# Half-row block ends, a spread gain row and other banks for the first gate unit, in a two-layer decoder on one core

## The chip, the cores and the metric

The kernel runs on one core of a Trainium2 chip. The metric is the device time in microseconds, from the launch of the program to its end; lower is better.

## What is computed

Two decoder layers on 256 tokens of width 1024, all weights read once from HBM in fp32. Layer 0 mixes with a state-space block, layer 1 with block attention on a shared K and V; each layer then has attention over 256 memory tokens and a gated feed-forward of width 2816.

```
x = x + rmsnorm(mixer(rmsnorm(x, mix_pre_g)), mix_post_g)
x = x + rmsnorm(memory_cross_attention(rmsnorm(x, mem_pre_g), mem_n, ...), mem_post_g)
x = x + rmsnorm(swiglu(rmsnorm(x, ffn_pre_g), w_gu, w_down), ffn_post_g)
```

So there are six places at which a product is normed, weighted with a post gain, added to x, and x is normed again with a pre gain for the next product. They are called block ends here: n = 0 to 5, behind w_out, wo0, down0, mo, wo1, down1. At n = 5 no second norm follows, and x goes out.

## The kernel before

The order on each engine is written out by hand, with semaphores between engines. Weights come in 1 MB units (128 x 2048 fp32) through a ring of four slots. For each unit SP issues the load when the unit four places back has been used (w_used), ScalarE rounds it to w_hi (L860), VectorE subtracts to w_lo (L1163, the weight remainder), and TensorE makes three products (hi x hi, hi x lo, lo x hi). Activations are split in the same way.

Tokens are two tiles of 128 (t = 0, 1). m_part() (L530) makes the product of a block end in banks 4 to 7, two banks of 512 columns for each token tile. The last two units are taken for tile 0 first, then for tile 1:

```
steps = [(i, t) for i in range(n - 2) for t in range(ST)] + [(i, t) for t in range(ST) for i in (n - 2, n - 1)]
```

norms() (L924) on ScalarE squares the product, sums it (statistic(), L880), and takes Ln and Exp. update() (L1219) on VectorE refines the inverse root in inverse_rms() (L1187), multiplies by it and by post_row (L1226), adds to x (L1229), raises x_ready, and calls normalise() (L1199), which needs the statistic of the new x and writes ntmp (L1205) for u_ready. TensorE transposes ntmp in turn() (L555, L567); ScalarE copies the result to actT_hi (L892) and VectorE makes actT_lo (L1213, raising turn_lo), and the next product waits for turn_lo (turn_done, L572).

While a block end runs, TensorE has fill work: units of the memory K and V of the same or the next layer, which do not depend on x. turn() takes one whole unit, the transposes of tile 0, half a unit, those of tile 1, and the other half. Ends 0 to 3 have two such units each, end 4 (wo1) has none. units_ahead() (L341) says how many units the engines prepare during an end: three, at end 4 two.

The feed-forward's gate and up units (pair_unit, L465) use two banks each, 0-1 for even and 2-3 for odd units, and loop_t() (L516) waits ahead of its loop until the two banks of the fill units have been copied out. A fill unit uses bank 0 or 1.

At the start SP loads both tiles of x, the first norm's gains spread over all partitions (512 KB written from 4 KB, into pre_row), the identity, and weights. TensorE runs dummy matmuls, warm() (L575), 40 before the first transposes and 24 behind them. d_pair is spread into par_rows on VectorE (L1249) ahead of the remainders of the first turn(). GpSimd issues the loads of later gain rows and, in the state-space part, sums squares. turn(1) (at L642) is the memory tokens' own norm, during the z units.

## Time and profile before

| | us |
|---|---|
| median of 3 runs (953.19 to 955.23) | 954.88 |
| the profiled execution: its time | 954.65 |
| its span, first to last instruction | 952.8 |
| TensorE busy in it | 921.3 |
| VectorE busy | 617.9 |
| ScalarE busy | 488.0 |
| mean granted TensorE clock, share of full speed | 0.990 |

The span is what the profile covers; 1.85 us of the execution's time lie around it. TensorE is the engine that is busy nearly always, so the time is its work and the gaps in it. The chain of work that ended last has 84% of the span on TensorE, 10% on VectorE and 4% on ScalarE. Idle time of the other engines matters only where TensorE waits for them.

### The profile page before, as it was taken

The numbers are of one execution on the slowest core, as the hardware profiler recorded it, in microseconds if no ns is written. First come the engines' busy times: TensorE is split into PE (matmuls) and PEld (weight loads), VectorE is DVE, ScalarE is ACT, GpSimd is POOL, SyncE is SP. The second block draws the span as 40 slices with busy tenths as digits, with TensorE's granted clock in tenths as the row PEclk, the third lists the DMA queues.
The fourth block names the chain that finished last, engine by engine and source line by source line (L and its number), as shares of the span: only waits on it lengthen the run. The fifth ranks groups of instructions, "written<-read, shape, count | busy, mean of one in ns | idle before, by whom it ended". The sixth has DMA issues, their size and how long they took to land.

```text
span 952.8 us, 14251 instructions
## 1 busy us (share of the span) xinstructions
PE 921.3 (97%) x5920; PEld 820.1 (86%) x5920; DVE 617.9 (65%) x689; ACT 488.0 (51%) x654; POOL 55.2 (6%) x67
## 2 busy tenths in 40 slices
PE   8999999999999999999999999999999599999996
PEld 6999998878899888888888999987998488888885
DVE  6788466895754677777643854675854657777533
ACT  5565467664555554444434644656645634444332
POOL 1000003450000000000000220000000000000000
PEclk9999999999999999999999999999999799999999
DMA  8756544225652555555555796434643345555551
GB/s 265 264 181 190 160 142 131 100 94 177 201 196 89 177 179 195 195 180 176 182 214 177 227 281 202 132 112 133 221 151 110 115 153 196 180 176 182 205 186 44
DMA packets 121060, 163.77 MB, mean 172 GB/s; under 512 B 4077, under 2 KB 106917, under 8 KB 121013
## 3 DMA queue, kind: packets, MB, share of 16 engines
q1 hardware_dynamic: 117684, 151.99, 48.8%
q0 software_dynamic: 3328, 11.10, 3.8%
q8 instruction: 35, 0.57, 0.3%
q14 instruction: 13, 0.10, 0.0%
HBM read 162.01 MB, written 1.07 MB: 171 GB/s over the span
## 4 chain that ended last, share of the span: by engine, by line
PE 84%; DVE 10%; ACT 4%; issue 1%; DMA 1%; SPq 0%; DVEq 0%; ACTq 0%
PE bank L450 49%; PE bank L471 18%; PE bank L473 9%; DVE w_lo L1163 2%; DVE ntmp L1226 1%; PE bank L772 1%; PE bank L743 1%; DVE x L1229 1%; DVE ntmp L1205 1%; ACT ntmp L882 1%; PE bank L661 1%; PE bank L567 1%; DMA d_pair<-in_ssm_d_dram 1%; DVE stats L1194 1%; DVE stats L1196 1%
## 5 line engine op out<-in xcount | busy, mean ns | idle before, releaser
L1163 DVE TENSOR_TENSOR w_lo<-w_raw,w_hi 128x2048 fp32r<-128x2048 f32 x135 | 308.7, 2292 | 134.8 <-ACT w_hi L860 134.1
L860 ACT ACTIVATE w_hi<-w_raw 128x2048 fp32r<-128x2048 f32 x135 | 257.3, 1913 | 207.6 <-DMA w_raw<-in_ffn_w_gu_dram 102.4
L471 PE MATMUL bank<-actT,w_hi 128*128 128x512 f32 x704 | 250.6, 401 | 2.6 <-DVE actT L1213 1.6
L450 PE MATMUL bank<-actT,w_hi 128*128 128x256 f32 x1152 | 209.3, 284 | 0.8 <-DVE w_lo L1174 0.5
L473 PE MATMUL bank<-actT,w_lo 128*128 128x256 f32 x704 | 198.4, 282 | 0.0
L450 PEld LDWEIGHTS bank<-actT,w_hi 128*128 128x128 f32 x1152 | 179.6, 192 | 2.3 <-issue 1.3
L471 PEld LDWEIGHTS bank<-actT,w_hi 128*128 128x128 f32 x704 | 133.1, 189 | 36.4 <-issue 3.1
L450 PE MATMUL bank<-actT,w_lo 128*128 128x256 f32 x576 | 163.0, 283 | 0.0
L473 PEld LDWEIGHTS bank<-actT,w_lo 128*128 128x128 f32 x704 | 133.9, 190 | 0.0
L450 PEld LDWEIGHTS bank<-actT,w_lo 128*128 128x128 f32 x576 | 110.5, 192 | 0.0
L450 PE MATMUL bank<-w_hi,hT_hi 128*128 128x512 f32 x176 | 68.5, 389 | 0.0
L450 PE MATMUL bank<-w_lo,hT_hi 128*128 128x512 f32 x176 | 68.5, 389 | 0.0
L450 PE MATMUL bank<-w_hi,hT_lo 128*128 128x512 f32 x176 | 68.5, 389 | 0.0
L450 PE MATMUL bank<-w_hi,actT 128*128 128x512 f32 (+1 forms) x256 | 64.1, 339 | 0.0
L1429 DVE TENSOR_REDUCE hval<-bank 128x512 f32<-128x1024 f32 x22 | 26.9, 1224 | 44.0 <-PE bank L473 44.0
L450 PEld LDWEIGHTS bank<-w_hi,actT 128*128 128x128 f32 x256 | 44.3, 190 | 5.4 <-issue 0.3
L450 PE MATMUL bank<-w_lo,actT 128*128 128x512 f32 (+1 forms) x128 | 43.0, 336 | 0.0
L450 PEld LDWEIGHTS bank<-w_hi,hT_lo 128*128 128x128 f32 x176 | 33.0, 188 | 7.0
L450 PEld LDWEIGHTS bank<-w_hi,hT_hi 128*128 128x128 f32 x176 | 33.0, 188 | 6.9
L450 PEld LDWEIGHTS bank<-w_lo,hT_hi 128*128 128x128 f32 x176 | 33.0, 188 | 6.8
L450 PE MATMUL bank<-w_hi,memT_hi 128*128 128x256 f32 x128 | 37.2, 290 | 0.0
L450 PE MATMUL bank<-memT_hi,w_hi 128*128 128x256 f32 x128 | 37.2, 290 | 0.0
(209 smaller groups left out, 1334.2 us busy)
## 6 DMA issues: line engine op xcount, KB each, us to landing
w_raw<-in_ffn_w_gu_dram SPq DMA_DIRECT2D x44, 1024.0 KB, 5.0
w_raw<-in_ffn_w_down_dram SPq DMA_DIRECT2D x22, 1024.0 KB, 4.9
w_raw<-in_ssm_w_in_dram SPq DMA_DIRECT2D x20, 1024.0 KB, 5.3
w_raw<-in_mem_w_kv_dram SPq DMA_DIRECT2D x16, 1024.0 KB, 5.3
w_raw<-in_ssm_w_out_dram SPq DMA_DIRECT2D x8, 1024.0 KB, 4.9
w_raw<-in_mem_w_q_dram SPq DMA_DIRECT2D x8, 1024.0 KB, 5.0
w_raw<-in_mem_w_o_dram SPq DMA_DIRECT2D x8, 1024.0 KB, 4.9
w_raw<-in_w_kv_dram SPq DMA_DIRECT2D x8, 1024.0 KB, 6.5
```

The source lines that it names most:

```text
L450: ins = pe.matmul(dst, a, b, start=first and n == 0, stop=last and n == len(passes) - 1, skip_group_check=True)
L471: pe.matmul(bank[:, b + c, :], wh, actT[:, k].rearrange("p e n -> p (e n)"), start=k == 0, stop=False, skip_group_check=True)
L473: ins = pe.matmul(bank[:, b + c, S:2 * S], wl, actT_hi[:, k, :], start=False, stop=k == KD - 1, skip_group_check=True)
L567: ins = pe.transpose(bank[:, 4 + 2 * t + half, q * P:(q + 1) * P], ntmp[:, t, c:c + P], ident)
L661: pe.matmul(bank[rows, 3 + j % 2 * 3, 0:S], xtok[:, j % 3, 0, rows], mt[:, j % 3, e, 0:S], start=True, stop=False, skip_group_check=True)
L743: ins = pe.matmul(bank[:, b, t * S:(t + 1) * S], qT[:, 2 * h + kk, t * P:(t + 1) * P], memK[:, 2 * h + kk, :], start=kk == 0, stop=kk == 1 ...
L772: ins = pe.matmul(bank[:, 2 + h % 2, d * S:(d + 1) * S], memV[:, m, c:c + P], probT[:, h % 2, m, :], start=m == 0, stop=m == 1, skip_group ...
L860: act.activation(hi[:, u % SLOTS, :], raw[:, u % SLOTS, :], ACT.Copy).then_inc(w_hi_done, 1)
L882: act.activation(ntmp[:, t, :], src, ACT.Square, accum_out=stats[:, 0, c:c + 1]).then_inc(sum_ready, 1)
L1163: dve.tensor_tensor(lo[:, s, :], raw[:, s, :], hi[:, s, :].bitcast(F32), ALU.subtract).then_inc(w_lo_done, 1)
L1194: own.mark(dve.scalar_tensor_tensor(out=step, in0=r, scalar=v, in1=r, op0=ALU.mult, op1=ALU.mult))
L1429: dve.tensor_reduce(dst[:, b], halves, AX.X, ALU.add).then_inc(t_out["dve"], 1)
```

## The change

- m_part: the last two units are taken in four quarters (tile 0 left half of the columns, tile 0 right half, tile 1 left, tile 1 right) of 12 matmuls each. m_quarter is raised behind the first three, w_used in the last.
- ScalarE: each square is done in two halves of 512 columns; the first half's sum goes through an added Identity, which gives its mean plus eps, and enters Ln as the bias. The copies of tile 0's transposes now stand ahead of the statistic of x of tile 1, and the third prepared unit behind all.
- VectorE: the product times post_row is made half by half, before the scale is known; one operation per half then multiplies by the scale and adds x. The remainders of tile 0's transposes stand ahead of the second norm of tile 1, and the third weight remainder behind it.
- turn on TensorE: half a unit of fill, tile 0, two halves of fill, tile 1, half a unit; the transposes wait half by half.
- The first norm's gains come as one row on one partition. Two matmuls with a row of ones spread them into banks 0 and 1, where the first norm reads them. The dummy matmuls are 24, 16 and 16. first_row and ones_row overlie conv_acc in the shared region, which stays at its address.
- d_pair is spread on GpSimd.
- Gate and up units use banks 2-3 for even and 0-1 for odd units. The wait for the last fill unit's copy is at the second unit.
- x is stored in four pieces of 256 KB, not in two of 512.
- At end 4 the table load for silu stands ahead of the last copies, not behind them.

Counts on x_ready, u_ready and sum_ready follow the halves. In the diff, removed lines of m_part, norms and the copy of d_pair, which the listing above has, are left out.

```diff
-WARM = [10, 6]
+WARM = [6, 4, 4]
...
+        first_row, _ = shared("first_row", [P, D], F32, 0)
+        ones_row, _ = shared("ones_row", [P, P], F32, 4096)
...
+        def sums_in(c, half):
+
+            return c + 1 if c < 4 else 2 * (c - 4) + 5 + half
...
             for t in range(ST):
                 sp.dma_start(x[:, t, :], A["x"][0, t * P:(t + 1) * P, :]).then_inc(x_loaded[t], 16)
-            sp.dma_start(pre_row[:], every_row(TURN_GAIN[0])).then_inc(pre_first, 16)
+                if t == 0:
+                    sp.dma_start(first_row[0:1, :], TURN_GAIN[0].unsqueeze(0)).then_inc(row_loaded, 16)
             sp.dma_start(const[:, 0:P], A["consts"][:, 0:P]).then_inc(ident_loaded, 16)
             load(0)
...
-                sp.wait_ge(x_ready, 2 * len(POST_GAIN) - 1 + t)
-                sp.dma_start(out[0, t * P:(t + 1) * P, :], x[:, t, :]).then_inc(stored, 16)
-            sp.wait_ge(stored, 16 * ST)
+                for half in range(2):
+                    sp.wait_ge(x_ready, 4 * (len(POST_GAIN) - 1) + 2 * t + half + 1)
+                    cols = slice(half * 512, half * 512 + 512)
+                    sp.dma_start(out[0, t * P:(t + 1) * P, cols], x[:, t, cols]).then_inc(stored, 16)
+            sp.wait_ge(stored, 16 * 2 * ST)
...
+            pool.wait_ge(par_loaded, 64)
+            d_rows = slice(D_ROW, D_ROW + XT)
+            pool.tensor_copy(par_rows[d_rows, 1, :].rearrange("c (e n) -> c e n", e=2), d_pair[d_rows, :].unsqueeze(2).broadcast_to([XT, 2, HD])).then_inc(consts_made, 1)
+            pool.wait_ge(u_ready, 4)
...
-                    pair_unit(u % SLOTS, i % 2 * 2).then_inc(w_used, 1)
+                    pair_unit(u % SLOTS, 2 - i % 2 * 2).then_inc(w_used, 1)
...
-                for e, n in FREED[v0 - 2:v0]:
-                    pe.wait_ge(t_out[e], n)
                 with pe.Fori(0, iters) as i:
                     for j in range(5):
+                        if j == 1:
+                            e, n = FREED[v0 - 1]
+                            pe.wait_ge(t_out[e], n)
                         if j:
                             pe.wait_ge(t_out["dve"], i * 4 + (d0 + j - 1))
                         if j < 4:
                             pe.wait_ge(w_lo_done, i * 4 + (u0 + j + 1))
-                            pair_unit((u0 + j) % SLOTS, j % 2 * 2).then_inc(w_used, 1)
+                            pair_unit((u0 + j) % SLOTS, 2 - j % 2 * 2).then_inc(w_used, 1)
...
+                def part(i, t, half, r):
+
+                    u, k = U[(name, i)], i * MR + r
+                    ah, al = act_hi[:, k, t * P:(t + 1) * P], act_lo[:, k, t * P:(t + 1) * P]
+                    cols = slice(r * D + half * 512, r * D + half * 512 + 512)
+                    wh, wl = hi[:, u % SLOTS, cols], lo[:, u % SLOTS, cols]
+                    return product(bank[:, 4 + 2 * t + half, :], [(ah, wh), (ah, wl), (al, wh)], k == 0, k == n * MR - 1)
+
+                for i in range(n - 2):
+                    ready(i)
+                    pe.wait_ge(w_lo_done, U[(name, i)] + 1)
+                    for t in range(ST):
+                        if t and i == 0 and last_y:
+                            last_y()
+                        for r in range(MR):
+                            for half in range(2):
+                                ins = part(i, t, half, r)
+                    ins.then_inc(w_used, 1)
+                for t in range(ST):
+                    for half in range(2):
+                        for i in (n - 2, n - 1):
+                            if t == 0 and half == 0:
+                                ready(i)
+                                pe.wait_ge(w_lo_done, U[(name, i)] + 1)
+                            for r in range(MR):
+                                ins = part(i, t, half, r)
+                            if t and half:
+                                ins.then_inc(w_used, 1)
+                        if not (t and half):
+                            ins.then_inc(m_quarter, 1)
...
-                if name:
-                    fill(name, i)
                 for t in range(ST):
-                    if name and t:
-                        fill_half(name, i + 1, 0)
-                    pe.wait_ge(u_ready, 2 * k + t + 1)
+                    if name:
+                        if t:
+                            fill_half(name, i, 1)
+                        fill_half(name, i + t, 0)
                     for half in range(2):
+                        pe.wait_ge(u_ready, 4 * k + 2 * t + half + 1)
                         for q in range(4):
                             c = (half * 4 + q) * P
...
+            pe.wait_ge(row_loaded, 16)
+            for half in range(2):
+                product(bank[:, half, :], [(ones_row[0:1, :], first_row[0:1, half * 512:(half + 1) * 512])], True, True).then_inc(pre_first, 1)
+            warm(WARM[1])
...
+            def statistic_halves(c, t, src, *ready):
+
+                first, first_mean = small[:, 2 + t:3 + t], small[:, 4 + t:5 + t]
+                for half, (s, count) in enumerate(ready):
+                    cols = slice(half * 512, half * 512 + 512)
+                    act.wait_ge(s, count)
+                    act.activation(ntmp[:, t, cols], src[:, cols], ACT.Square,
+                                   accum_out=stats[:, 0, c:c + 1] if half else first).then_inc(sum_ready, 1)
+                    act.wait_ge(sum_ready, sums_in(c, half))
+                    if half == 0:
+                        own.mark(act.activation(first_mean, first, ACT.Identity, bias=eps_col, scale=1.0 / D))
+                own.wait()
+                own.mark(act.activation(stats[:, 1, c:c + 1], stats[:, 0, c:c + 1], ACT.Ln, bias=first_mean, scale=1.0 / D))
+                own.wait()
+                act.activation(stats[:, 2, c:c + 1], stats[:, 1, c:c + 1], ACT.Exp, scale=-0.5).then_inc(stat_ready, 1)
...
-                act.wait_ge(m_half, n + 1)
-                hi_upto(last + 2)
+                statistic_halves(stat_col(n, 0, 0), 0, msum[0], (m_quarter, 3 * n + 1), (m_quarter, 3 * n + 2))
+                if units_ahead(n) > last + 2:
+                    hi_upto(last + 2)
                 if POST_TURN[n] is not None:
-                hi_upto(units_ahead(n))
+                    statistic_halves(stat_col(n, 0, 1), 0, x[:, 0, :], (x_ready, 4 * n + 1), (x_ready, 4 * n + 2))
+                statistic_halves(stat_col(n, 1, 0), 1, msum[1], (m_quarter, 3 * n + 3), (w_used, last + 1))
                 if POST_TURN[n] is not None:
+                    turn(POST_TURN[n], actT_hi, [0])
+                    statistic_halves(stat_col(n, 1, 1), 1, x[:, 1, :], (x_ready, 4 * n + 3), (x_ready, 4 * n + 4))
+                if units_ahead(n) > last + 2:
+                    hi_upto(units_ahead(n))
...
-                act.preload_act_table_set("silu_and_others")
+                if layer == 0:
+                    act.preload_act_table_set("silu_and_others")
...
             norms(4)
-            turn(7, actT_hi)
+            act.preload_act_table_set("silu_and_others")
+            turn(7, actT_hi, [1])
...
+                t = (c - 4) % 4 // 2 if c < 24 else c - 24
+                total0, v0 = small[:, 2 + t:3 + t], small[:, 6 + t:7 + t]
+                dve.wait_ge(sum_ready, sums_in(c, 0))
+                if c < 4:
+                    own.mark(dve.tensor_scalar(v, total, -0.5 / D, -0.5 * EPS, ALU.mult, ALU.add))
+                else:
+                    own.mark(dve.tensor_scalar(v0, total0, -0.5 / D, -0.5 * EPS, ALU.mult, ALU.add))
+                    if gains:
+                        gains(0)
+                    dve.wait_ge(sum_ready, sums_in(c, 1))
+                    own.wait()
+                    own.mark(dve.tensor_scalar(v, total, -0.5 / D, v0, ALU.mult, ALU.add))
+                    if gains:
+                        gains(1)
...
-                dve.scalar_tensor_tensor(out=ntmp[:, t, :], in0=src[:, t, :], scalar=stats[:, 5, c:c + 1],
-                                         in1=pre_row[:], op0=ALU.mult, op1=ALU.mult).then_inc(u_ready, 1)
-
-            def turn(k, dst_hi, dst_lo):
-                for t in range(ST):
+                    dve.wait_ge(*((pre_loaded, 16 * k) if k else (pre_first, 2)))
+                for half in range(2):
+                    cols = slice(half * 512, half * 512 + 512)
+                    dve.scalar_tensor_tensor(out=ntmp[:, t, cols], in0=src[:, t, cols], scalar=stats[:, 5, c:c + 1],
+                                             in1=pre_row[:, cols] if k else bank[:, half, :], op0=ALU.mult, op1=ALU.mult).then_inc(u_ready, 1)
+
+            def turn(k, dst_hi, dst_lo, tokens=range(ST)):
...
+                    def gains(half):
+
+                        cols = slice(half * 512, half * 512 + 512)
+                        own.mark(dve.tensor_tensor(ntmp[:, t, cols], bank[:, 4 + 2 * t + half, :], post_row[:, cols], ALU.mult))
+
+                    inverse_rms(c, gains)
+                    for half in range(2):
+                        cols = slice(half * 512, half * 512 + 512)
+                        dve.scalar_tensor_tensor(out=x[:, t, cols], in0=ntmp[:, t, cols], scalar=stats[:, 5, c:c + 1],
+                                                 in1=x[:, t, cols], op0=ALU.mult, op1=ALU.add).then_inc(x_ready, 1)
+                    if t and POST_TURN[n] is not None:
+                        turn(POST_TURN[n], actT_hi, actT_lo, [0])
+                    if t == 0 and units_ahead(n) > last_unit(M_OF_POST[n]) + 2:
+                        lo_upto(last_unit(M_OF_POST[n]) + 2)
                     if POST_TURN[n] is not None:
                         normalise(POST_TURN[n], stat_col(n, t, 1), t, x)
+                if units_ahead(n) > last_unit(M_OF_POST[n]) + 2:
+                    lo_upto(units_ahead(n))
...
-            dve.wait_ge(par_loaded, 64)
...
+            lo_upto(U[("mq", 1)])
...
```

Place 1, VectorE, block end 0, tile 1 of the tokens from the sum of the product to the new x. Before:

```order
L1191 TENSOR_SCALAR stats<-stats 128x1 [waits sum_ready]
L1194 SCALAR_TENSOR_TENSOR stats<-stats 128x1 [waits stat_ready,dve_step]
L1196 TENSOR_SCALAR stats<-stats 128x1 [waits dve_step]
L1226 SCALAR_TENSOR_TENSOR ntmp<-bank,stats,post_row 128x1024 [waits dve_step]
L1229 TENSOR_TENSOR x<-x,ntmp 128x1024 [waits dve_step]
L1163 TENSOR_TENSOR w_lo<-w_raw,w_hi 128x2048 [waits w_hi_done]
```

After:

```order
L1241 TENSOR_SCALAR small<-small 128x1 [waits sum_ready]
L1288 TENSOR_TENSOR ntmp<-bank,post_row 128x512
L1246 TENSOR_SCALAR stats<-stats,small 128x1 [waits dve_step,sum_ready]
L1288 TENSOR_TENSOR ntmp<-bank,post_row 128x512
L1251 SCALAR_TENSOR_TENSOR stats<-stats 128x1 [waits stat_ready,dve_step]
L1253 TENSOR_SCALAR stats<-stats 128x1 [waits dve_step]
L1293 SCALAR_TENSOR_TENSOR x<-ntmp,stats,x 128x512 [waits dve_step]
L1293 SCALAR_TENSOR_TENSOR x<-ntmp,stats,x 128x512
L1272 TENSOR_TENSOR actT<-bank,actT 128x4x128 [waits turn_hi] x2
```

The two operations of 1024 columns have become four of 512, of which the two on post_row no longer wait for the scale (stat_ready). The weight remainder (w_lo) is gone from here, and the remainders of tile 0's transposes have come in behind x.

Place 2, VectorE, what follows there: the second norm of tile 1 and the remainders of the transposes. Before:

```order
L1191 TENSOR_SCALAR stats<-stats 128x1 [waits sum_ready]
L1194 SCALAR_TENSOR_TENSOR stats<-stats 128x1 [waits stat_ready,dve_step]
L1196 TENSOR_SCALAR stats<-stats 128x1 [waits dve_step]
L1205 SCALAR_TENSOR_TENSOR ntmp<-x,stats,pre_row 128x1024 [waits dve_step]
L1213 TENSOR_TENSOR actT<-bank,actT 128x4x128 [waits turn_hi] x4
```

After:

```order
L1241 TENSOR_SCALAR small<-small 128x1 [waits sum_ready]
L1246 TENSOR_SCALAR stats<-stats,small 128x1 [waits dve_step,sum_ready]
L1251 SCALAR_TENSOR_TENSOR stats<-stats 128x1 [waits stat_ready,dve_step]
L1253 TENSOR_SCALAR stats<-stats 128x1 [waits dve_step]
L1264 SCALAR_TENSOR_TENSOR ntmp<-x,stats,pre_row 128x512 [waits dve_step]
L1264 SCALAR_TENSOR_TENSOR ntmp<-x,stats,pre_row 128x512
L1208 TENSOR_TENSOR w_lo<-w_raw,w_hi 128x2048 [waits w_hi_done]
L1272 TENSOR_TENSOR actT<-bank,actT 128x4x128 [waits turn_hi] x2
```

The weight remainder that stood ahead of this norm now stands between it and the last two remainders of the transposes.

Place 3, TensorE, the start of the program (cum is a tile of zeros, const the identity). Before:

```order
L577 UNCONDITIONAL_BRANCH [waits zeros_made]
L579 MATMUL bank<-cum_102 128x256 x4
L577 REGISTER_ALU
L577 COMPARE_AND_BRANCH
L567 MATMUL bank<-const,ntmp 128x128 [waits u_ready,ident_loaded]
L567 MATMUL bank<-const,ntmp 128x128 x7
L567 MATMUL bank<-const,ntmp 128x128 [waits u_ready]
L567 MATMUL bank<-const,ntmp 128x128 x7
L588 MATMUL bank<-const,par_rows 128x128 [waits consts_made]
```

After:

```order
L603 MATMUL bank<-cum_104 128x256 x4
L601 REGISTER_ALU
L601 COMPARE_AND_BRANCH
L463 MATMUL bank<-first_row,ones_row 128x512 [waits row_loaded]
L463 MATMUL bank<-first_row,ones_row 128x512
L601 UNCONDITIONAL_BRANCH
L603 MATMUL bank<-cum_104 128x256 x4
L601 REGISTER_ALU
L601 COMPARE_AND_BRANCH
L591 MATMUL bank<-const,ntmp 128x128 [waits u_ready,ident_loaded]
L591 MATMUL bank<-const,ntmp 128x128 x3
L591 MATMUL bank<-const,ntmp 128x128 [waits u_ready]
```

Two matmuls on the row of gains stand among the dummy ones, and the transposes wait once per half row.

## Rows read from the trace of the kernel before

**Rows 1.** The page, part 1: engine, busy us, share, instructions.

```profile
PE 921.3 (97%) x5920; PEld 820.1 (86%) x5920; DVE 617.9 (65%) x689; ACT 488.0 (51%) x654; POOL 55.2 (6%) x67
```

**Rows 2.** The waits of TensorE: us in total, times, longest.

```profile
PE bank L567 <- DVE ntmp L1205: 16.8, 9, 5.1
...
PE bank L471 <- ACT memK L913: 1.0, 1, 1.0
```

**Rows 3.** Timeline, first block end: start us, us, engine, line, names, idle before.

```profile
238.33 2.29 DVE L1163 TENSOR_TENSOR w_lo<-w_raw,w_hi 128x2048 fp32r<-128x2048 f32 x1 [3.21 <-ACT w_hi L860]
...
247.76 1.03 ACT L882 ACTIVATE ntmp<-bank 128x1024 f32<-128x1024 f32 x1 [2.25 <-PE bank L450]
...
248.90 0.15 DVE L1191 TENSOR_SCALAR stats<-stats 128x1 f32<-128x1 f32 x1 [2.38 <-ACT ntmp L882]
...
252.50 2.29 DVE L1163 TENSOR_TENSOR w_lo<-w_raw,w_hi 128x2048 fp32r<-128x2048 f32 x1
...
253.00 0.28 PE L450 MATMUL bank<-w_hi,memT_hi 128*128 128x256 f32 x1
...
255.39 1.28 DVE L1205 SCALAR_TENSOR_TENSOR ntmp<-x,stats,pre_row 128x1024 f32<-128x1024 f32 x1
...
258.75 1.03 PE L567 MATMUL bank<-const,ntmp 128*128 128x128 f32 x8
...
263.96 1.09 PE L567 MATMUL bank<-const,ntmp 128*128 128x128 f32 x8 [1.31 <-DVE ntmp L1205]
```

**Rows 4.** Timeline of TensorE, first gate unit of the first layer.

```profile
344.07 0.49 PE L471 MATMUL bank<-actT,w_hi 128*128 128x512 f32 x1 [0.97 <-ACT memK L913]
```

**Rows 5.** Timeline of TensorE, block end of wo1 (no fills).

```profile
748.35 1.68 PE L567 MATMUL bank<-const,ntmp 128*128 128x128 f32 x8 [3.11 <-DVE ntmp L1205]
755.12 1.97 PE L567 MATMUL bank<-const,ntmp 128*128 128x128 f32 x8 [5.10 <-DVE ntmp L1205]
758.67 0.79 PE L471 MATMUL bank<-actT,w_hi 128*128 128x512 f32 x1 [1.58 <-DVE actT L1213]
```

**Rows 6.** Timeline of the tail, and one window: busy by engine, clock, DMA, GB/s.

```profile
944.88 1.02 ACT L882 ACTIVATE ntmp<-bank 128x1024 f32<-128x1024 f32 x1 [3.76 <-PE bank L450]
...
948.48 1.23 DVE L1229 TENSOR_TENSOR x<-x,ntmp 128x1024 f32<-128x1024 f32 x1
...
949.74 0.36 SPq L386 DMA_DIRECT2D out_dram<-x  x1
...
951.00:952.00 1.00, 0.00 (x0) 0.00 (x0) 0.00 (x0) 0.00 (x0) 0.00 (x0) 0.50 0.86 348
```

**Rows 7.** Timeline and one window of the start, and timeline round turn(1).

```profile
6.64 0.21 DVE L1196 TENSOR_SCALAR stats<-stats 128x1 f32<-128x1 f32 x1
...
7.96 1.28 DVE L1205 SCALAR_TENSOR_TENSOR ntmp<-x,stats,pre_row 128x1024 f32<-128x1024 f32 x1 [1.11 <-DMA pre_row<-in_mix_pre_g_dram]
...
9.39 1.07 PE L567 MATMUL bank<-const,ntmp 128*128 128x128 f32 x8 [1.82 <-DVE ntmp L1205]
...
12.00:15.00 3.00, 3.00 (x17) 2.43 (x16) 2.76 (x6) 2.58 (x4) 0.00 (x0) 0.53 1.10 337
...
12.21 0.22 DVE L1249 COPY par_rows<-d_pair 16x128 f32<-16x128 f32 x1 [1.08 <-DMA d_pair<-in_ssm_d_dram]
...
17.27 0.50 PE L450 MATMUL bank<-actT,w_hi 128*128 128x256 f32 x2 [0.48 <-DVE w_lo L1174]
...
114.90 1.09 PE L567 MATMUL bank<-const,ntmp 128*128 128x128 f32 x8 [0.73 <-DVE ntmp L1205]
...
123.36 0.48 PE L450 MATMUL bank<-actT,w_hi 128*128 128x256 f32 x2 [0.33 <-DVE w_lo L1163]
```

**Rows 8.** Groups by shape: count, busy us, mean ns, idle before.

```profile
L1213 DVE TENSOR_TENSOR actT<-bank,actT 128x512 fp32r<-128x512 f32 x28 | 17.9, 684 | 2.4 <-ACT actT L892 2.3
...
L892 ACT ACTIVATE actT<-bank 128x512 fp32r<-128x512 f32 x28 | 15.2, 597 | 12.4 <-PE bank L567 12.4
...
L424 POOL TENSOR_TENSOR ysum<-ysum,ysq 128x256 f32<-128x256 f32 x12 | 14.1, 1177 | 0.9
```

80 lines of the change are left out of this document (22 added, 58 removed).

## The prediction

> **What bounds the kernel now.** I read five views in this order: the page, the waits of TensorE, the timeline round each place where TensorE waited, the windows with the granted clock, and the groups by shape. The page has TensorE busy for 921.3 us of a span of 952.8 [rows 1]. The matmuls themselves are the same before and after the change, so what it can win is in the remaining 31.5 us, plus the stretches in which TensorE counts as busy on dummy matmuls or at half clock. The waits say where that idle time is: 16.8 us in nine waits for the normalised rows that turn() transposes, and 1.0 us for a copy out of bank 1 [rows 2]. The rest is the first microseconds, the last ones, and scraps.
>
> The timeline of the first block end shows what such a wait is made of [rows 3]. ScalarE squares token tile 0 at 247.76, and VectorE has the sum at 248.90. Then come VectorE's scaled row, the addition, and the weight remainder of a prefetched unit (2.29), and only then the normalised row at 255.39. Token tile 1 goes through the same chain behind it. TensorE arrives with its fill work done and stands 1.31 us at 263.96. The same 1.31 us recur at the three other block ends that have fill work: with 1.82 and 0.73 at the start, 0.73 at turn(1) and the 3.11 and 5.10 below, four of 1.31 make up the 16.8 us.
>
> Where there is no fill work (before the second feed-forward) the chain is bare: waits of 3.11, 5.10 and 1.58 us [rows 5]. At the very end nothing covers it either [rows 6].
>
> **Prices.** An elementwise VectorE operation of 512 columns takes 0.68 us and a ScalarE one 0.60 [rows 8]; of 1024 columns they take 1.28 and 1.03 [rows 3]. Halving therefore costs about 0.08 us extra on VectorE for each cut where operations follow without a wait, and I use 0.74 for a half with a scalar operand (0.68 and a little, as the scalar form stands 0.05 above the other at 1024 columns: 1.28 against 1.23 [rows 3, 6]). The sum of the last half row comes 0.43 us sooner than that of a whole row (1.03 less 0.60): 0.72 us after the square starts, against 1.14 [rows 3].
>
> **A block end with fills (four of them).** I count from the moment at which the last square of tile 0 can start, 247.76 in rows 3. Before, the post-gain product and the addition were two 1024-column operations behind the statistic. Now the gain product runs while ScalarE does Ln and Exp, and one fused operation per half finishes x. VectorE: sum 0.72, gain product of the second half to 1.5, two Newton steps to 2.0, x halves ready at 2.75 and 3.4. Then the weight remainder, which keeps its place, to 5.6, the second norm's scalars to 6.4, and the normalised halves at 7.1 and 7.8. TensorE reaches tile 0's transposes after the rest of its matmuls (253.00, which is 5.24) and now only half a unit of fill, 2.87 (a whole one took from 253.00 to 258.75 [rows 3]): at 8.1. So it waits for nothing, with 1.0 us to spare.
>
> Tile 1 on VectorE: two gain halves, scalars and x to 11.2, the two remainders of tile 0's transposes to 12.4, scalars to 13.3, and the first half of the normalised row at 14.1. TensorE is there at 8.1 + 1.05 + 5.75 = 14.9. The 1.31 us wait goes, with 0.8 us to spare. What is late next: the weight remainder that the change puts behind this row (2.29) stands on VectorE ahead of the last two remainders of the transposes, which end at 18.2. TensorE has finished its last half unit at 18.8. Spare 0.6 us. That unit's load is released some 1.3 us later than before (half a quarter), because unit n-2 now ends in the last quarter; the remainder made of it stands some 10 us behind the release. The last unit's own remainder is needed 1.3 us earlier too, 4 us before 247.4, and it was done at 240.6 [rows 3]. **4 x 1.31 = 5.2 us gained.** Bounds: 0 (spare used up) and 5.2, since TensorE can't gain more than it waited.
>
> **First gate unit in other banks.** It no longer waits for the copy of k1's second unit. That wait was 0.97 [rows 4]. About 0.1 of it is loop entry that stays. **0.85 us gained**, bounds 0.5 and 0.97. For the second layer there is no such copy, so nothing. One wait now stands inside the loop; its value is long reached, so it costs nothing.
>
> **The block end without fills.** The same chain from 739.8: normalised tile 0 at 746.1 and 746.8 instead of 748.3; tile 1's halves at 753.1 and 753.8 instead of 755.07. TensorE is at half clock here, 1.97 us for eight transposes against 1.07 at the start [rows 5, 7], and I leave that so, since it idles between the tiles as long as before. The last four transposes end at 754.9, copy and remainder add 1.4, and the first gate matmul starts at 756.55 against 758.67. The moved table load falls into a wait. **2.1 us gained**, bounds 1.3 and 3.
>
> **The tail.** From the square at 944.88 the last half of x is done at 948.3, against 949.71, when the whole row was [rows 6]. The last store then carries 256 KB, not 512, and the store moved 348 GB/s: 0.75 us less. **2.15 us gained**, bounds 1.4 (store no shorter) and 2.3.
>
> **The start.** VectorE had the scale of tile 0 at 6.85 and stood until 7.96 for the row of gains on all partitions [rows 7]. Now 4 KB are loaded, one place earlier in SP's queue, and two matmuls spread them into banks 0 and 1, between 24 and 16 dummy matmuls; before there were 40. Normalised halves at 7.6 and 8.3, tile 1's at 9.6 and 10.3. Then the remainders, which stood behind the copy of d_pair until 12.4 [rows 7], run from 10.2 to 12.7. Weight halves on both engines follow, and the first real matmul could start at 15.1 instead of 17.27. The copy of d_pair goes to GpSimd, behind four DMA issues and that same load. It cost 0.22 on VectorE [rows 7]; on GpSimd I bound it by 0.22 and 1.18 [rows 8] and take 0.5. If d_pair lands as before (12.2), par_rows are turned at 13.2, 16 dummy matmuls end at 15.3, and the first real matmul is at 15.4. I take that: **1.9 us gained**, bounds 0 and 2.3.
>
> **The middle.** turn(1) waited 0.73 for tile 1 of mem and 0.33 later for a remainder [rows 7]. The first shrinks, but the second is the end of a ScalarE and VectorE chain from the same starting point, which the halving lengthens: **0.1 us lost**, bounds 0.3 lost and 0.3 gained. Elsewhere the queue of SP is not changed. On GpSimd the gain rows' DMAs wait for the same events in other counts, and the new copy stands only ahead of a DMA that waits until w_used 3.
>
> **Sum.** 5.2 + 0.85 + 2.1 + 2.15 + 1.9 - 0.1 = 12.1. The profiled execution took 954.65 us, the median of the runs shown is 954.88, within their spread. 954.65 - 12.1 = **942.6 us**.
>
> **Rivals.**
> 1. The start gives nothing. The par_rows transposes and dummy matmuls stand on TensorE ahead of the first real one, and GpSimd may reach the copy late. TensorE's clock is at stake too: it ran at 0.53 of full speed from 12 to 15 [rows 7], after TensorE had stood 1.82 us at 9.39. Now it may stand behind tile 1 instead, and a fall that came three microseconds later would lie on real matmuls. For 3.4 us at half speed that costs 1.7. Against it: less idle time in all. Time: 942.6 + 1.9, up to + 3.6: 944.5 to 946.2. The Trainium skill (TensorE: Matmul & The Clock Gate, What's actually happening) has the throttled clock as the default and activity as what releases it; by that, moving the idle time moves the slow stretch, as this rival has it.
> 2. The waits come back at the block ends: the half of the fill that now stands behind tile 0's transposes no longer covers them, or VectorE's last remainders come after the fill. A spare of 0.6 to 1.0 us is small against a chain of some 20 operations. If each operation there is 0.1 us longer than I have it, each of the four ends loses up to 1.2 us: 942.6 + 4.8 = 947.4 at most, 945 likely.
> 3. Slower than before. VectorE's chain per end has eleven operations that are now half rows. If a half row costs e more than 0.74 us, TensorE waits 11e - 0.6 at each of four ends, 11e at the fifth, and the tail grows by 3e: 58e - 2.4 in all. This eats the gain of 12.1 from e = 0.25, a half row at 0.99 us. At e = 0.5, where a half costs nearly what a whole row does, the time is 954.65 - 12.1 + 26.6 = 969. Against it: 28 such operations at 0.684 [rows 8]; for it only that the fused form with x as both input and output, and a product straight from PSUM, are not in the trace at this width. The Trainium skill (VectorE: DVE Perf Modes, The TRN2 errata) speaks against such cuts: each instruction pays a fixed latency that a large tile pays once. Its formula for fp32 tensor_tensor gives 0.69 us at 512 columns, beside the row's 0.684, so by it e is zero.
> 4. The change does little of what it says: a wait that ended last at the four ends and in the feed-forward comes back as another one of the same length, and only tail and start remain: 954.65 - 4.05 = 950.6. For it: three engines take part in each end and the trace shows only the wait that ended last. One part of the change's name does nothing in any case: no tile after the new ones has another address.
>
> **How the numbers follow.** My forecast 0.62, rival 1 0.15, rival 2 0.15, rival 3 0.03, rival 4 0.03, and 0.02 for no change at all. The range runs down to 940.5 (all terms at their better bound) and up to 947.2, where rivals 1 and 2 end. What lies outside is the far part of rival 2, rival 3, rival 4, and my own terms if several are off the same way: 2 in 10. About 0.2% (1.9 us) is what a measurement here can tell from no change. Faster 0.95, same 0.02, slower 0.03.
>
> **What would show it.** In the profile after: no wait for the normalised row above 0.2 us at the four ends, first gate matmul straight behind its fill, first gate matmul of layer two about 2 us sooner after the last one of wo1, last store under 2.5 us before the span's end, first real matmul at 15.4. VectorE's half rows must stand at 0.68 to 0.75. If they stand at 0.9 or more, or TensorE waits for turn_lo, I am wrong in rivals 3 or 2.

## The result, and the profile after

The changed kernel took 943.16 us (median of four runs, 940.91 to 945.87) beside 955.06 for the kernel before (four runs, 953.19 to 955.90): a ratio of 0.9889, 95% interval 0.9867 to 0.9911 (the two medians by themselves give 0.9875). I had forecast 942.6. The profiled execution took 943.9, 10.75 less than the one before; its span is 942.1. The sum agrees, and yet two of its terms were far off, and an effect that it did not have made up for most of that.

The page, part 1, and the waits of TensorE, which answer to [rows 1] and [rows 2] (us in total, times, longest):

```profile
PE 920.4 (98%) x5916; PEld 819.3 (87%) x5916; DVE 624.7 (66%) x751; ACT 499.6 (53%) x720; POOL 55.6 (6%) x68
```

```profile
PE bank L591 <- DVE ntmp L1264: 7.6, 4, 5.8
PE bank L463 <- DVE w_lo L1219: 2.1, 1, 2.1
...
PE bank L484 <- DVE actT L1272: 1.6, 1, 1.6
```

Nine waits of 16.8 us for the normalised row have become four of 7.6. The 1.0 for memK is gone, and the wait for a weight remainder ahead of the first real matmul has grown from 0.48 [rows 7] to 2.06. The timeline of the first block end (start us, us, engine, line, names, idle before), to be held against [rows 3]:

```profile
247.58 0.60 ACT L914 ACTIVATE ntmp<-bank 128x512 f32<-128x512 f32 x1 [1.39 <-PE bank L463]
...
254.20 1.42 DVE L1264 SCALAR_TENSOR_TENSOR ntmp<-x,stats,pre_row 128x512 f32<-128x512 f32 x2
...
255.69 1.03 PE L591 MATMUL bank<-const,ntmp 128*128 128x128 f32 x8
...
261.36 1.42 DVE L1264 SCALAR_TENSOR_TENSOR ntmp<-x,stats,pre_row 128x512 f32<-128x512 f32 x2
...
262.31 1.16 PE L591 MATMUL bank<-const,ntmp 128*128 128x128 f32 x8
```

Neither group of transposes has idle time in front, where the second had 1.31. But the eight transposes of tile 1 took 1.16 us, those of tile 0 1.03: the second half row came at 262.8 and the last four waited for it a little. At the ends 2 and 3 it is 1.32; before the change it was 1.09 at all four. The gate units, the end without fills and the tail, against [rows 4 to 6]:

```profile
340.32 0.49 PE L484 MATMUL bank<-actT,w_hi 128*128 128x512 f32 x1
...
740.51 1.32 PE L591 MATMUL bank<-const,ntmp 128*128 128x128 f32 x8 [1.10 <-DVE ntmp L1264]
747.67 1.97 PE L591 MATMUL bank<-const,ntmp 128*128 128x128 f32 x8 [5.83 <-DVE ntmp L1264]
751.22 0.79 PE L484 MATMUL bank<-actT,w_hi 128*128 128x512 f32 x1 [1.59 <-DVE actT L1272]
...
936.11 0.60 ACT L914 ACTIVATE ntmp<-bank 128x512 f32<-128x512 f32 x1 [1.70 <-PE bank L463]
...
938.96 0.99 SPq L396 DMA_DIRECT2D out_dram<-x  x2
```

Two stores are one row there; the second was issued at 939.63, 2.48 us before the span's end (before: 3.08). The start, against [rows 7]:

```profile
1.74 4.92 PE L603 MATMUL bank<-cum 128*128 128x256 bf16 x24 [1.74 <-DVE small L1314]
6.59 1.98 PE L463 MATMUL bank<-first_row,ones_row 1*128 1x512 f32 x4
...
7.09 1.06 ACT L926 ACTIVATE ntmp<-x 128x1024 f32<-128x1024 f32 x1 [1.11 <-DMA x<-in_x_dram]
...
8.68 1.41 DVE L1264 SCALAR_TENSOR_TENSOR ntmp<-x,stats,bank 128x512 f32<-128x512 f32 x2 [2.12 <-PE bank L463]
...
16.83 0.51 PE L463 MATMUL bank<-actT,w_hi 128*128 128x256 f32 x2 [2.06 <-DVE w_lo L1219]
```

VectorE stood 2.12 us, not for a DMA but for the two products that spread the row. They are four records, 1.98 us, and they began only when 24 dummy matmuls had ended at 6.59.

Laid over each other, the two profiles give the gain stage by stage. The same event came sooner by 0.44 us at the first real matmul (17.27, now 16.83) and 0.18 at the first square of the first block end (247.76, 247.58), so the middle lost 0.26. At the last wo1 matmul it is 5.82 (744.85, 739.03): less 0.18, and less 0.9 for the first gate unit, the four ends with fills gave 4.7. When VectorE begins to reduce layer two's first gate unit it is 6.51 (766.26, 759.75): 0.69 for the end without fills. At the last of layer two's 22 gate and up units it is **8.75** (884.98, 876.23): 2.24 us came from the gate loop, in which the matmuls and their order were not changed, only the banks. The tail gave 1.94.

That loop is the surprise. VectorE reduces each unit when TensorE has finished it. After the change, the reductions of the third and the twenty-first unit of layer one, and of the first and the last unit of layer two:

```profile
357.72 1.22 DVE L1497 TENSOR_REDUCE gate<-bank 128x512 f32<-128x1024 f32 x1
...
459.48 1.22 DVE L1497 TENSOR_REDUCE gate<-bank 128x512 f32<-128x1024 f32 x1
...
759.75 1.22 DVE L1497 TENSOR_REDUCE gate<-bank 128x512 f32<-128x1024 f32 x1 [3.16 <-PE bank L486]
...
876.23 1.23 DVE L1497 TENSOR_REDUCE hval<-bank 128x512 f32<-128x1024 f32 x1 [1.89 <-PE bank L486]
```

The same four in the kernel before:

```profile
361.46 1.22 DVE L1429 TENSOR_REDUCE gate<-bank 128x512 f32<-128x1024 f32 x1
...
463.22 1.21 DVE L1429 TENSOR_REDUCE gate<-bank 128x512 f32<-128x1024 f32 x1
...
766.26 1.22 DVE L1429 TENSOR_REDUCE gate<-bank 128x512 f32<-128x1024 f32 x1 [3.41 <-PE bank L473]
...
884.98 1.22 DVE L1429 TENSOR_REDUCE hval<-bank 128x512 f32<-128x1024 f32 x1 [2.09 <-PE bank L473]
```

Layer one: (459.48 - 357.72) / 18 is 5.65 us a unit, and so is (463.22 - 361.46) / 18. Layer two: (876.23 - 759.75) / 21 is 5.55, where (884.98 - 766.26) / 21 is 5.65. A unit has 16 pairs of one 512-column and one 256-column matmul; the time from pair to pair, 353.3 or 346.7 ns, is called the slow and the quick rhythm below.

### The profile page after: what moved, and what is told of

Same layout as the page of the kernel before. It is cut to its first block, busy times and chain, and to the rows that moved or that the text cites. A ratio compares the mean times of both kernels' runs of the same rounds, so it can differ in the third digit from the quotient of the medians.

```text
span 942.1 us, 14413 instructions
## 1 busy us (share of the span) xinstructions
PE 920.4 (98%) x5916; PEld 819.3 (87%) x5916; DVE 624.7 (66%) x751; ACT 499.6 (53%) x720; POOL 55.6 (6%) x68
## 3 DMA queue, kind: packets, MB, share of 16 engines
q0 software_dynamic: 3328, 11.10, 3.6%
## 4 chain that ended last, share of the span: by engine, by line
PE 87%; DVE 7%; ACT 3%; issue 2%; DVEq 0%; ACTq 0%
PE bank L463 51%; PE bank L484 18%; PE bank L486 9%; DVE conv_acc L1378 2%; DVE w_lo L1208 2%; PE bank L800 1%; PE bank L771 1%; PE bank L591 1%; PE bank L689 1%; DVE ntmp L1264 1%; PE bank L603 1%; PE bank L854 1%; PE bank L844 0%; PE bank L727 0%; ACT w_hi L888 0%
```

## The experiments

Unless an edit says otherwise, each is made in the changed kernel, so it is compared with 943.16 (and with the 942.65 of the first experiment). A ratio is that to the kernel before, run beside it.

**1. The same kernel again.** No edit.

> The changed kernel, nothing altered. In its profile 32 matmuls of a gate unit came in pairs 346.7 ns apart in the second layer's gate loop and 353.3 ns apart in the first layer's (before the change: 353.3 in both). That is 0.106 us a unit, 2.2 us over the 21 units, which no term of my sum has. Theory A (the rhythm is set by the program: by the bank order or by how TensorE comes out of the half clock there): the pairs stand again at 353 in the first and 347 in the second layer, and the total within 1 us of 943.2. Theory B (the rhythm is a state that an execution falls into by the instant at which the loop is entered): the profile shows another combination, 347/347 or 353/353, with a span 2.2 us shorter or longer by it, and the single times spread over 4 to 5 us as before (940.9 to 945.9), in steps of about 2.2.

Measured: 942.65 us (six runs, 940.53 to 946.19), ratio 0.9883 (0.9858 to 0.9908). Its units took 5.55 us in both layers: theory B, as far as the combination changed; that the instant of entry picks it is not shown. Its start and its clock differ from the first profile too. The window is: busy by engine, granted clock, DMA share, GB/s.

```profile
17.23 0.54 PE L463 MATMUL bank<-actT,w_hi 128*128 128x256 f32 x1 [2.06 <-DVE w_lo L1219]
```

```profile
17.30:20.70 3.40, 3.40 (x16) 3.40 (x17) 2.01 (x5) 3.40 (x2) 0.00 (x0) 0.50 0.84 231
744.40:754.50 10.10, 5.87 (x20) 4.90 (x21) 7.36 (x12) 8.50 (x11) 0.45 (x1) 0.50 0.21 76
```

After 2.06 us of idle time the clock fell to the lower of its two levels (0.50, 1.2 GHz) just as the first real matmuls began. From there to the wait behind turn(1) this execution took 107.81 us, the first one 106.35: 1.5 us given away. My rival 1 described this; of the eight profiles with this start it happened in this one alone. The second window is the end without fills: there the clock was back at full 10.24 us after its fall, where the first profile needed 13.65. From the last wo1 matmul to the reduction of the first gate unit this execution took 19.87 us, the first one 20.72.

**2. The spread ahead of the dummy matmuls.** WARM counts them in groups of four.

```
-WARM = [6, 4, 4]
+WARM = [2, 8, 4]
...
-                if t == 0:
-                    dve.wait_ge(*((pre_loaded, 16 * k) if k else (pre_first, 2)))
+                if t == 0 and k:
+                    dve.wait_ge(pre_loaded, 16 * k)
                 for half in range(2):
+                    if t == 0 and not k:
+                        dve.wait_ge(pre_first, half + 1)
```

> The two matmuls that spread the row of gains stand behind 8 dummy matmuls, not 24 (then 32 more), and each half of tile 0 waits for its own half of the row. My theory: the start missed 1.5 of the 1.9 us I gave it because VectorE stood 2.12 us for the spread, which began at 6.59 behind dummy matmuls at half clock and took 1.98. By it VectorE starts the normalised row at 6.6 to 7.1 instead of 8.68 and the first real matmul is at 15.3 to 15.9 instead of 16.83, if tile 1 isn't last; where tile 1 of x is (it landed at 7.09, its scale at 9.2), the gain is smaller, about 0.9: 15.9. Rival: the row itself lands late, the spread can't start before 5.5, and the products run at half clock at 3.4 us for four: the normalised row at 8.5 or later, the first real matmul where it was, 16.8, or later. In us: 942.3 (mine), 943.2 or slower (rival).

Measured: 943.78 us (five runs, 943.76 to 945.48), ratio 0.9894. The rival's time, and a start worse than it had it:

```profile
4.13 3.78 PE L463 MATMUL bank<-first_row,ones_row 1*128 1x512 f32 x4 [0.52 <-DMA first_row<-in_mix_pre_g_dram]
7.83 5.84 PE L603 MATMUL bank<-cum 128*128 128x256 bf16 x32
13.51 1.91 PE L591 MATMUL bank<-const,ntmp 128*128 128x128 f32 x16
...
19.61 0.50 PE L463 MATMUL bank<-actT,w_hi 128*128 128x256 f32 x2 [2.22 <-DVE w_lo L1219]
```

The row had landed by 4.13, so the DMA is not late. But the four records took 3.78 us at the lower clock, and the clock rose only at 12.32 (in the thirteen other profiles of this study between 4.4 and 7.4). 32 dummy matmuls, most of them at half clock, then stood in front of tile 0's transposes. The start lost 2.8 us against the first profile; the total hardly moved because both gate loops of this profile had the quick rhythm, worth 2.2. Before the clock rose, TensorE had run 8 dummy matmuls, stood idle 0.52 us, run the four one-row products, and then run dummy matmuls for 4.5 us. The Trainium skill (TensorE: Matmul & The Clock Gate, What's actually happening) makes activity the thing that releases the clock; the trace agrees in so far as the rise came while matmuls ran. Why it came so late here this one profile does not show.

**3. The row loaded onto all partitions again.**

```
-WARM = [6, 4, 4]
+WARM = [10, 0, 4]
...
-                if t == 0:
-                    sp.dma_start(first_row[0:1, :], TURN_GAIN[0].unsqueeze(0)).then_inc(row_loaded, 16)
+            sp.dma_start(pre_row[:], every_row(TURN_GAIN[0])).then_inc(row_loaded, 16)
...
-            pe.wait_ge(row_loaded, 16)
-            for half in range(2):
-                product(bank[:, half, :], [(ones_row[0:1, :], first_row[0:1, half * 512:(half + 1) * 512])], True, True).then_inc(pre_first, 1)
-            warm(WARM[1])
...
```

> The start undone but for the copy on GpSimd: the row of gains is loaded onto all partitions in the third place of the queue, 40 dummy matmuls in one piece, no spread. My theory, by which the spread and the copy's move between them gave 0.44 us: VectorE starts the normalised row at about 8.0, so 0.7 sooner than with the spread, but the second tile and par_rows come from the queue behind 512 KB; first real matmul at 17.0 plus or minus 0.3, so +0.2 us against the change. Rival (the spread cost more than it saved): 16.3 or sooner, 0.5 us faster than the change. Second rival (the move of the copy cost what the spread gave): above 17.3.

Measured: 942.29 us (five runs, 940.38 to 945.78), ratio 0.9872, no different from the change. VectorE and TensorE:

```profile
8.47 0.75 DVE L1259 SCALAR_TENSOR_TENSOR ntmp<-x,stats,pre_row 128x512 f32<-128x512 f32 x1 [1.76 <-DMA pre_row<-in_mix_pre_g_dram]
```

```profile
16.64 0.38 PE L462 MATMUL bank<-actT,w_hi 128*128 128x256 f32 x1 [1.30 <-DVE w_lo L1214]
```

The first real matmul came between what my theory and the first rival said: the spread neither saves nor costs anything that can be told (16.64 against 16.83 and 17.23 in the two profiles of the change, whose clock also rose later). By elimination the start owes its gain to the rest, the half rows and the copy of d_pair off VectorE; no run parts these two.

**4. TensorE kept busy at the end without fills.** The matmuls stand in turn(7), between the two tiles.

```
+                    if t and busy:
+                        stay_busy(busy)
...
+            def stay_busy(n):
+
+                with pe.Fori(0, n):
+                    for _ in range(4):
+                        pe.matmul(bank[:, 2, 0:S], const[:, 0:P // 2].bitcast(BF16), const[:, 0:P].bitcast(BF16), start=True, stop=True,
...
-            turn(7)
+            turn(7, busy=11)
```

> 44 dummy matmuls (128 x 256, bf16) between the transposes of tile 0 and tile 1 at the block end without fills, where TensorE stands 5.83 us and its clock is at half from 743.44 to 757.09. At 0.12 us each, as at the start, they take 5.3 us of the 5.8. Theory A (the idle time makes the clock fall, and half a clock on the first nine pairs of the gate unit is what took back the gain of that end): the clock stays at full, eight transposes take 1.05 instead of 1.97 us, nine pairs save 0.29 us each, 2.7 us, and the first gate matmul is about 1.0 us sooner: 3.6 us faster, 939.6. Theory B (the clock falls all the same, or the dummy matmuls come in the way of the transposes): no gain or up to 1 us lost. Beside it, on the rhythm of the pairs in the second layer: if what makes it 347 ns is the way out of the half clock, it is 353 here, and 2.2 us of the gain go, 941.8.

Measured: **938.81 us** (six runs, 937.33 to 945.25), ratio 0.9843 (0.9813 to 0.9873); beside it experiment 1 had 942.65.

```profile
740.70 4.97 PE L602 MATMUL bank<-const 128*128 128x256 bf16 x44
746.70 1.32 PE L593 MATMUL bank<-const,ntmp 128*128 128x128 f32 x8 [1.03 <-DVE ntmp L1273]
749.60 0.49 PE L484 MATMUL bank<-actT,w_hi 128*128 128x512 f32 x1 [1.58 <-DVE actT L1281]
```

```profile
743.50:757.00 13.50, 10.88 (x71) 9.07 (x70) 10.90 (x15) 9.86 (x14) 0.53 (x1) 1.00 0.24 80
```

Theory A. From the last wo1 matmul to the first gate unit's reduction it takes 17.38 us (738.07 to 755.45), where the change took 20.72 in its first profile and 19.87 in its second: 3.3 or 2.5 gained. The rhythm in the second layer stayed the quick one, so it does not come from leaving the lower clock. One of the six runs took 945.25 at a mean clock of 0.994, the others had 0.999. The later experiments 9 to 11 have this edit too, and there the clock still fell, for 3.41 us.

**5. Gate matmuls grouped.**

```
                     for k in range(KD):
                         cols = slice(k * TC + c * P, k * TC + (c + 1) * P)
-                        wh, wl = hi[:, slot, cols], lo[:, slot, cols]
-                        pe.matmul(bank[:, b + c, :], wh, actT[:, k].rearrange("p e n -> p (e n)"), start=k == 0, stop=False,
+                        pe.matmul(bank[:, b + c, :], hi[:, slot, cols], actT[:, k].rearrange("p e n -> p (e n)"), start=k == 0, stop=False,
                                   skip_group_check=True)
-                        ins = pe.matmul(bank[:, b + c, S:2 * S], wl, actT_hi[:, k, :], start=False, stop=k == KD - 1,
+                    for k in range(KD):
+                        cols = slice(k * TC + c * P, k * TC + (c + 1) * P)
+                        ins = pe.matmul(bank[:, b + c, S:2 * S], lo[:, slot, cols], actT_hi[:, k, :], start=False, stop=k == KD - 1,
                                         skip_group_check=True)
```

> In a gate unit the eight 512-column matmuls of a half stand first and the eight 256-column ones behind them, where the changed kernel lets them alternate. Five profiles so far show the alternating pair at either 353.3 or 346.7 ns, in each layer by itself: 353/347, 347/347, 347/347, 353/353, 353/347. Runs of equal matmuls elsewhere stand at 226.7 and 120 ns, 346.7 together. Theory A (the slow rhythm belongs to the alternation, and which one an execution has is chance of the instant): grouped, every unit takes 16 x 0.3467 = 5.55 us in both layers, the single times lie within 2 us where they lay over 5 to 6, and the median is 1 to 2 us below the 942.7 of the unaltered kernel. Theory B (the slow rhythm is in the loop, its loads or VectorE's and ScalarE's use of the banks): 5.65 us a unit still turns up in some layer, and the spread stays.

Measured: 943.1 us (six runs, 941.41 to 944.01), ratio 0.9893. The spread halved from 5.7 us to 2.6, the median did not move. Two units in a row took 11.17 us throughout, 5.587 each: behind every change from 256 to 512 columns the next few matmuls take up to 9 ns more each. That lies between the two rhythms of the alternating form (5.547, 5.654), so theory A holds for the cause and not for the gain. Over the twelve profiles of alternating kernels, before and after, 12 layers had the quick rhythm and 12 the slow one.

**6. Banks of the gate units as before.**

```
-                    pair_unit(u % SLOTS, 2 - i % 2 * 2).then_inc(w_used, 1)
+                    pair_unit(u % SLOTS, i % 2 * 2).then_inc(w_used, 1)
...
+                for e, n in FREED[v0 - 2:v0]:
+                    pe.wait_ge(t_out[e], n)
                 with pe.Fori(0, iters) as i:
                     for j in range(5):
-                        if j == 1:
...
```

> The banks of the gate units as before the change: the first gate unit of layer one writes banks 0 and 1 and waits for the copy of k1's second unit out of bank 1. My theory: that wait comes back at 0.9 to 1.0 us in layer one, nothing in layer two, so 0.9 us slower than the change by the profile's stages. Rival (the new order of the last half units has moved the copy out of the way, so the wait is hidden anyway): 0.3 or less. Second rival (bank order, not the wait, makes the quick rhythm of the second layer): pairs at 353 ns in both layers, 2.2 us slower.

Measured: 944.37 us (four runs, 941.84 to 945.94), ratio 0.9897.

```profile
340.46 0.49 PE L484 MATMUL bank<-actT,w_hi 128*128 128x512 f32 x1 [0.97 <-ACT memK L956]
```

The wait is back at its old 0.97. From the first real matmul to the reduction of the twenty-first unit this profile took 443.54 us, the change 442.65: 0.89, as forecast. Its rhythm is slow in both layers, as the second rival has it, but so was that of experiment 3 with the new banks; one profile does not settle it.

**7. The whole fill unit ahead of tile 0 again.**

```
-                    if name:
-                        if t:
-                            fill_half(name, i, 1)
-                        fill_half(name, i + t, 0)
+                    if name and t == 0:
+                        fill_half(name, i, 0)
+                        fill_half(name, i, 1)
+                    elif name:
+                        fill_half(name, i + 1, 0)
```

> The fill work at the four ends stands as before the change (a whole unit ahead of tile 0's transposes, half a unit between the tiles, half behind), all half rows stay. TensorE's matmuls and their number are the same. Theory A (the gain of the ends needs the earlier transposes of tile 0, because ScalarE copies them ahead of tile 1's second square): from A, the square of tile 0, TensorE is at tile 0's transposes at +11.1 instead of +8.1, ScalarE's two copies end at +12.9, the squares, Ln and Exp of tile 1 behind them at +14.8, and tile 1's normalised half at +15.9, where TensorE arrives at +14.7: 1.2 to 1.9 us waited at each of the four ends, 5 to 7 us slower in all. Theory B (shorter links alone make the gain, and the place of the fill doesn't matter): no wait above 0.3, same time as the change.

Measured: 951.08 us (ten runs, 948.62 to 954.23), ratio 0.9969 (0.9952 to 0.9987): some 8 us slower. ScalarE and TensorE:

```profile
258.43 1.09 ACT L937 ACTIVATE actT<-bank 128x512 fp32r<-128x512 f32 x2 [4.42 <-PE bank L592]
259.40 0.63 ACT L915 ACTIVATE ntmp<-x 128x512 f32<-128x512 f32 x1
```

```profile
263.05 1.32 PE L592 MATMUL bank<-const,ntmp 128*128 128x128 f32 x8 [1.35 <-DVE ntmp L1265]
```

Theory A. ScalarE's copies of tile 0 stand ahead of tile 1's second square, and behind a late transpose they push it. 1.35 us of wait return here, and each of the four ends is 1.35 to 1.65 us longer by the stages, 6.1 in all: more than the 4.7 that the four ends had gained. Half rows with TensorE's old order lose there, while ScalarE keeps its new one, with the copies ahead of the second square; half rows with both old orders were not run. The rest of the 8 us I can't place; its gate loops ran slow and quick like the change's.

**8. One more half-row product ahead of x of tile 1.**

```
                     inverse_rms(c, gains)
+                    if t:
+                        gains(1)
+                        own.wait()
```

> One more half-row product (0.68 us, the second gain product done twice) and its wait, some 0.72 us, on VectorE ahead of x of tile 1 at every end. Theory A (my forecast's spare of 0.8 us at tile 1 and 0.6 behind it is real): nothing at the four ends with fills, 0.7 at the one without, 0.7 in the tail: 1.4 us slower. Theory B (what the trace after shows: tile 1's eight transposes took 0.92 to 1.07 us in place of 0.79, so TensorE already stood 0.1 to 0.3 us for the second half, and the spare is gone): 0.6 to 0.7 at each of the four as well: 4.2 us slower.

Measured: 945.21 us (four runs, 944.51 to 946.36), ratio 0.9916.

```profile
262.72 1.32 PE L591 MATMUL bank<-const,ntmp 128*128 128x128 f32 x8 [0.41 <-DVE ntmp L1264]
```

0.41 us of wait, and 0.4 to 0.7 us more at each of the five ends and 0.7 in the tail by the stages, 3.4 in all. That is near theory B: the spare of 0.8 us that I had seen at tile 1 is 0 to 0.3. The medians differ by only 2.1 to 2.6; the rhythm, which was quick in both layers of this profile, blurs them.

**9. The first unit started on its first half.** With experiment 4's edit in it. The first four units leave the loop for this.

```
+                        if middle and c == 0 and k == KD // 2:
+                            middle()
...
+            for j in range(4):
+                if j == 2:
+                    pe.wait_ge(t_out["dve"], 1)
+                pe.wait_ge(*((w_lo_done, u0 + j + 1) if j else (first_lo, 1)))
+                t_unit((u0 + j) % SLOTS, j, actT_hi, actT_lo,
+                       middle=None if j else lambda: pe.wait_ge(w_lo_done, u0 + 1)).then_inc(w_used, 1)
...
+                if u == 0 and part == 0:
+                    ins.then_inc(first_lo, 1)
```

> The changed kernel with the 44 dummy matmuls at the end without fills, and with the first unit's matmuls waiting for the remainder of its first half only (the other half before its fifth row block). In the profiles so far the first real matmul stands 2.06 us idle for the remainder of the whole unit, whose first half is done 1.13 us sooner. Theory: it starts at 14.9 to 15.0 where the clock rises near 4.5 (16.0 to 16.1 without this edit), 1.1 us faster than wo1_busy, and with the idle time down to 0.9 us no half clock on real matmuls (which the unaltered kernel had in one profile, 17.30 to 20.72). Median 937.7. Rival: the second half's remainder is late for the fifth block (1.4 us after the start), so 0 to 0.3 of it comes back as a wait in the unit.

Measured: 941.3 us (four runs, 940.13 to 942.54), ratio 0.9859 (0.9836 to 0.9882). The start is as expected, the total is not:

```profile
15.06 0.36 PE L463 MATMUL bank<-actT,w_hi 128*128 128x256 f32 x1 [1.02 <-DVE w_lo L1237]
```

```profile
748.80:752.10 3.30, 3.30 (x11) 2.82 (x12) 2.56 (x2) 3.30 (x3) 0.00 (x0) 0.50 0.02 5
```

Both layers had the slow rhythm, 2.2 us against experiment 4's profile. And the clock fell once more: at 748.77, after 1.59 us of idle time and 0.1 us into the first gate matmul, for 3.41 us. That took back 1.6 of the 3.3 us (19.02 from the last wo1 matmul to the reduction).

**10. Each half of tile 0 waits for its half of the row.** With the edits of 4 and 9.

```
-WARM = [6, 4, 4]
+WARM = [6, 1, 5]
...
-                if t == 0:
-                    dve.wait_ge(*((pre_loaded, 16 * k) if k else (pre_first, 2)))
+                if t == 0 and k:
+                    dve.wait_ge(pre_loaded, 16 * k)
                 for half in range(2):
+                    if t == 0 and not k:
+                        dve.wait_ge(pre_first, half + 1)
```

> As parts_busy, and at the start each half of tile 0 waits for its own half of the spread row, with 4 dummy matmuls behind the spread in place of 16 and 20 in place of 16 behind the transposes. Theory A (VectorE's wait for the spread, 2.1 us, is on the path to the first matmul): the first normalised half starts 0.9 us sooner, tile 0's transposes follow it, and the first real matmul comes 0.3 to 0.9 us sooner than in parts_busy, the more the earlier x's tile 1 is there. Theory B (tile 1 of x, landing at 6.6 to 7.1, and its chain set the end): no gain. Rival C: with fewer dummy matmuls in a row the clock rises later or falls again before the real ones, 0.5 to 2 us slower, as when the spread stood early.

Measured: **937.79 us** (five runs, 936.73 to 940.09), ratio 0.9831 (0.9809 to 0.9852), the lowest of the study.

```profile
7.65 1.54 DVE L1286 SCALAR_TENSOR_TENSOR ntmp<-x,stats,bank 128x512 f32<-128x512 f32 x2 [1.16 <-PE bank L463]
```

```profile
14.89 0.36 PE L463 MATMUL bank<-actT,w_hi 128*128 128x256 f32 x1 [0.58 <-DVE w_lo L1237]
```

The first real matmul is at 14.89 though the clock rose at 5.81; experiment 8 with the same rise (5.95) had it at 16.73, of which 1.1 is experiment 9's. So theory A, 0.7. Against experiment 9's profile the start is only 0.2 sooner, and 4.5 of the 4.9 us between the spans are the rhythm (quick in both layers here). The clock fell at the first gate matmul here too (18.95 us from the last wo1 matmul to the reduction). That it is better than 4 or 9 by itself is therefore not shown. That it is better than the change is: the intervals of the two (0.9809 to 0.9852, and 0.9867 to 0.9911 or 0.9858 to 0.9908) don't meet.

**11. All of it with the grouped units.** Edits of 4, 5 and 9.

> As parts_busy, with the gate units' matmuls grouped (eight of 512 columns, then eight of 256). Grouped units took 5.587 us in both layers; alternating ones 5.50, 5.53, 5.547 or 5.654 by the execution. Theory: 937.7 plus or minus 0.5 in the median as parts_busy, with a spread of 3 us or less over the executions where parts_busy has 5 or more. If the median were 1 us or more above parts_busy's, the quick rhythms are the common ones and grouping costs.

Measured: 940.75 us (four runs, 940.50 to 941.48), ratio 0.9860. The spread is 1 us. The 5.50 and 5.53 us a unit in that expectation were my miscount: they came from experiment 8's profile, where a late reduction stood at the start of the stretch; two units in a row took 11.09 to 11.10 there, the quick rhythm. The median is 3 us above my figure and level with experiment 9's. In its profile, too, the clock fell ahead of the first gate matmul (18.79 us from the last wo1 matmul to the reduction), which the figure of 937.7 had not reckoned with.

**12. Whole stores at the end.**

```
-                for half in range(2):
-                    sp.wait_ge(x_ready, 4 * (len(POST_GAIN) - 1) + 2 * t + half + 1)
-                    cols = slice(half * 512, half * 512 + 512)
-                    sp.dma_start(out[0, t * P:(t + 1) * P, cols], x[:, t, cols]).then_inc(stored, 16)
-            sp.wait_ge(stored, 16 * 2 * ST)
+                sp.wait_ge(x_ready, 4 * (len(POST_GAIN) - 1) + 2 * t + 2)
+                sp.dma_start(out[0, t * P:(t + 1) * P, :], x[:, t, :]).then_inc(stored, 16)
+            sp.wait_ge(stored, 16 * ST)
```

> The changed kernel with one store of a whole token tile (512 KB) at the end in place of two of half rows. From the issue of the last store to the end of the span it was 3.08 us before the change and 2.48 after. My forecast gave the halving of the store 0.75 us; by the two profiles it is 0.60. So the last store is issued at the same distance from the last matmul (3.9 us) and the span ends 3.1 us behind it: 0.6 us slower in that stretch. Rival (two stores in flight share the queues, and the halving is worth nothing): 2.5 us.

Measured: 943.35 us (four runs, 942.71 to 945.59), ratio 0.9893.

```profile
937.85 0.36 SPq L394 DMA_DIRECT2D out_dram<-x  x1
```

The span is 940.9, so it ends 3.06 us behind the issue where the change has 2.48: 0.58, as expected. It is too small to see in the medians.

## Why the prediction was right, and where it was not

**Four ends, 5.2: right, measured 4.7.** All four 1.31 us waits are gone, and the normalised halves of tile 0 and 1 were done 7.4 and 14.5 us after the square against my 7.1 and 14.1. The 0.8 us of spare that I gave tile 1 is not there (experiment 8), and the transposes of tile 1 take 1.16 to 1.32 us where they took 1.09, which is the half microsecond. Rival 2 pointed there; of its 4.8 us at most, about 0.5 came. What I had taken for incidental, that tile 0 is transposed earlier, is the part without which, with the rest of the change as it is, the gain turns into a loss (experiment 7).

**First gate unit, 0.85: right**, 0.9 by the stages and 0.89 by undoing it.

**End without fills, 2.1: mis-sized, 0.7 in this profile.** The chain came near: first gate matmul 12.19 us after the last wo1 matmul began, 13.82 before, 1.6 sooner where I had 2.1. The step that failed is "TensorE is at half clock here, [...] and I leave that so". I counted the lower clock for the transposes alone. The stretch at half clock was 13.65 us long in both profiles (743.44 to 757.09, and 748.69 to 762.34). With the first gate matmul at 751.22, 5.9 us of it lay on real matmuls, where 3.7 had. A pair takes 0.64 us there and 0.35 at full clock, so coming sooner gave about 1 us back. How long the stretch is varies, though: it was 10.24 us in experiment 1, the same kernel, and by that profile the end gains 1.5 us (19.87 against the 21.41 of the one profile before). In the seven profiles with this end it took 19.9 to 20.7 us. Experiment 4 shows the whole price of the lower clock there: 2.5 to 3.3 us.

**Tail, 2.15: right, 1.94.** 4.83 to 3.49 us from the last square to the last half of x, 1.34 of my 1.4; the store 0.60 in place of 0.75 (0.58 by experiment 12). The 348 GB/s that I used was the mean of one microsecond; 256 KB in 0.60 us are 435.

**Start, 1.9: mis-sized, 0.44 in this profile.** My step had the spread row ready with the scale at 6.85. I had put no price on the spread itself, which takes 1.98 us at full clock, nor on the 24 dummy matmuls in front of it, which take 4.9 us when most of them run at the lower clock. In the trace they stand 0.213 us apart before the clock rises and 0.109 behind that. How many stand before it is not the same in each execution:

```
clock rose at   4.38   4.55   4.61   4.66   4.81   5.95   6.16   7.06
first matmul   15.96  16.05  16.07  16.10  16.17  16.73  16.83  17.23
```

(experiments 4, 12, 6, 7, 5, 8, the first profile, experiment 1; all with the change's start). Each microsecond by which the clock rises later moves the first real matmul 0.47 later. In the profile before, the clock rose at 4.58 and the matmul came at 17.27. At the same rise the change gains 1.2 us, as far as one profile of the kernel before can tell, so the first profile was an unlucky one by 0.75. Rival 1 was partly right: the clock does fall over real matmuls behind the start, in one profile of eight.

**Middle, -0.1:** -0.26. The wait for tile 1 of mem shrank as said, and the chain behind it grew.

**Rival 3, the slower one: wrong.** The half rows took 0.68 and 0.75 us, as costed.

**What the sum left out** is the rhythm of the gate loop, 2.24 us in the gain of this profile. The terms as measured are 4.74 + 0.90 + 0.69 + 1.94 + 0.44 - 0.26 = 8.45, and with 2.24 for the rhythm this is the measured 10.7. So the median lay within 0.6 us of the forecast partly by luck: the shortfall of 3.7 us in the terms was met to more than half by an effect that I did not have. With equal rhythm and an equal rise of the clock at the start, the two profiles would stand 9.2 us apart, and with experiment 1's shorter stretch at half clock at the end without fills 10.1. The ratio of 0.9889 is 10.6 us; over all 41 runs of the kernel before and all ten of the change the means stand 10.9 us apart, the medians of the first four of each 11.9, and the interval runs from 8.5 to 12.7. So little or nothing is missing; what the rest is, if there is one, is open (see the last section).

## What to carry to other kernels

When a stage is shortened in which TensorE idles long enough for its clock to fall, ask where the slow stretch will lie afterwards: filling that idle time with throwaway matmuls was worth 2.5 to 3.3 us where the clock then held, more than shortening the chain (0.7 to 1.5). It did not always hold: with a different start (experiments 9 to 11) it fell for 3.41 us in all three profiles, and about half of that gain was lost. A change of order can be the condition under which smaller pieces pay: with the fill work put back in its old place, the same half rows took 6 us longer. And take two profiles of one kernel before explaining the last 2 us between two kernels.

## What the runs showed that I had not expected

Alternating 512- and 256-column matmuls run in one of two rhythms for a whole loop: pairs 346.7 ns apart or 353.3. It changed between executions of the same kernel and between the two loops of one execution, with twelve loops of each in the twelve profiles, all at full clock but for the first pairs of layer two. Two kernels that differ in nothing can so differ by 4.5 us here. What picks the rhythm was not found. Both occur with the new bank order and behind the same entry into the loop. With the old bank order the two profiles (before, experiment 6) have the slow one in all four layers; but single runs of these kernels took 5.2 and 3.7 us less than the profiled one (949.42 and 954.65, 941.84 and 945.58), more than their clock can give: the mean clocks of each pair differ by 0.001 (0.991 and 0.990, 0.994 and 0.993), which I estimate at 2 us at most. So the quick one seems to occur there too, though no profile shows it. Whether it is rarer there is open; if it is, part of the gain in the medians would be rhythm. Sorted by width (experiment 5) the loop has one rhythm, between the two.

The clock rose at a different time in each execution, between 4.4 and 7.4 us, with the same dummy matmuls from 1.74 on, and at 12.32 where products of a single row of weights stood early among them. The stretch at half clock at wo1's end was 13.65 or 10.24 us long with the same kernel, and with the idle time mostly filled there was none in one profile and one of 3.41 in three.
